# RWKV-7 block inverses: 64-column products and transposes in place of the second product

## The reference

```python
def step(S, inp):
    r_t, w_t, k_t, v_t, a_t, b_t = inp
    sa = jnp.einsum('bhvk,bhk->bhv', S, a_t)
    S = S * w_t[:, :, None, :] + sa[..., None] * b_t[:, :, None, :] + v_t[..., None] * k_t[:, :, None, :]
    return S, jnp.einsum('bhvk,bhk->bhv', S, r_t)
```

## Time and profile before

| | |
|---|---|
| median of 3 runs | 1586.68 us (1586.61 to 1587.28) |
| the profiled execution, its own time | 1589.47 us |
| its span, first to last instruction | 1587.7 us |
| PE busy | 1506.8 us, 95% |
| PE weight loads busy | 1377.6 us, 87% |
| DVE / ACT busy | 980.5 us / 697.7 us |
| stretch of the 24 steps | about 158.75 to 257 us of the span |

### The profile page before, as it was taken

One profiled execution on the slowest core, in us unless ns is written; L12 is line 12 of the kernel. 1 busy time (PEld: TensorE's weight loads), 2 busy tenths in 40 slices (PEclk: granted clock), 3 DMA queues, 4 the chain that ended last, 5 costly groups with the idle time before them and its releaser, 6 DMA issues. The chain is left out here.

```text
span 1587.7 us, 26386 instructions
## 1 busy us (share of the span) xinstructions
PE 1506.8 (95%) x10462; PEld 1377.6 (87%) x10462; DVE 980.5 (62%) x1605; ACT 697.7 (44%) x1125; POOL 55.5 (3%) x85
## 2 busy tenths in 40 slices
PE   6889999999999999999889999999999998899998
PEld 6786899789999899989868999989998987699997
DVE  4775464776666766664357766676665454576665
ACT  5461445454434433456345443353443445454343
POOL 1021000000000000000000000000000000000000
PEclk9999999999999999999989999999999899999999
DMA  7331200165543554433405555445454331165440
GB/s 312 120 120 45 115 2 1 43 264 198 196 173 147 199 196 174 186 120 143 176 1 199 204 193 198 175 163 199 180 199 159 132 144 56 40 239 199 182 174 27
DMA packets 24640, 237.88 MB, mean 150 GB/s; under 512 B 2528, under 2 KB 4720, under 8 KB 5744
## 3 DMA queue, kind: packets, MB, share of 16 engines
q1 hardware_dynamic: 22032, 233.46, 39.1%
q10 hardware_dynamic: 2528, 3.32, 0.6%
HBM read 235.70 MB, written 1.07 MB: 149 GB/s over the span
## 5 line engine op out<-in xcount | busy, mean ns | idle before, releaser
L375 PE MATMUL ps<-uT_h,w_gu 128*128 128x256 f32 x3520 | 614.3, 280 | 0.3 <-DVE w_gu L1677 0.2
L375 PEld LDWEIGHTS ps<-uT_h,w_gu 128*128 128x128 f32 x3520 | 537.7, 188 | 11.1 <-issue 1.6
L375 PE MATMUL ps<-uT_l,w_gu 128*128 128x256 f32 x1760 | 478.8, 279 | 0.0
L375 PE MATMUL ps<-w_dn,h_r 128*128 128x512 f32 x1320 | 326.3, 396 | 3.3 <-DVE h_r L1716 2.2
L375 PEld LDWEIGHTS ps<-uT_l,w_gu 128*128 128x128 f32 x1760 | 325.5, 188 | 0.0
L375 PEld LDWEIGHTS ps<-w_dn,h_r 128*128 128x128 f32 x1320 | 239.4, 188 | 54.5 <-issue 4.9
L1119 ACT CAST w_gu<-ring 128x2048 fp32r<-128x2048 f32 x110 | 209.9, 1908 | 158.5 <-PE ps L375 157.4
L1677 DVE TENSOR_TENSOR w_gu<-ring,w_gu 128x2048 fp32r<-128x2048 f32 x110 | 252.1, 2292 | 36.0 <-ACT w_gu L1119 36.0
L1707 DVE TENSOR_TENSOR us<-ps,bc 128x256 f32<-128x256 f32 x110 | 46.6, 423 | 205.2 <-PE ps L375 205.1
L375 PE MATMUL ps<-wk 128*128 128x128 f32 (+4 forms) x940 | 145.4, 301 | 15.3 <-ACT wk L1239 3.8
L1132 ACT ACTIVATE wk<-wk 128x256 f32<-128x256 f32 x110 | 46.1, 419 | 256.5 <-DVE wk L1705 256.5
(11 more groups left out here) (325 smaller groups left out, 1808.4 us busy)
## 6 DMA issues: line engine op xcount, KB each, us to landing
ring<-wstream SPq DMA_DIRECT2D x145, 1536.0 KB, 6.3
cst<-consts_in SPq DMA_DIRECT2D x1, 2057.0 KB, 15.6
wk<-t_row ACTq DMA_DIRECT2D x1, 2048.0 KB, 7.9
wk<-masks_in SPq DMA_DIRECT2D x1, 1152.0 KB, 25.7
x<-x_in SPq DMA_DIRECT2D x2, 512.0 KB, 4.6
inh<-gains ACTq DMA_DIRECT2D x2, 512.0 KB, 8.5
out_dram<-x SPq DMA_DIRECT2D x4, 256.0 KB, 2.2
cst<-consts_in ACTq DMA_DIRECT2D x1, 146.0 KB, 4.3
```

Source lines behind the costliest of these rows:

```text
L375: return pe.matmul(o, l, r, start=start, stop=stop, skip_group_check=True)
```

## The change

The first product streams only 64 of M's 128 columns, those of the even blocks of the level, and writes them side by side into 256 columns of bank 0; ACT copies 256 columns. The product for `Mm` is formed from these 64 columns, and DVE puts it into the even blocks' columns of `Mm`. The product for `Mt` is gone at five of the six levels. In its place PE transposes the updated `Mm` of the quad one step later, in steps q = 1 to 20, and DVE copies the transposes over `Mt` without a mask. At the last level (q = 20 to 23) only `Mt` is needed: its one 64x64 block comes from a product with 64 weight columns and 64 moving columns, and a plain copy. Two semaphores are new, `MT_ps` (PE to DVE, transposes done) and `Mt_ready` (DVE to PE, copy done).

```diff
+LAST_LEVEL = (LEVELS - 2) * QUADS
+        def blocks(a, q):
+            return a.rearrange("p (j w n) -> p j w n", w=2, n=2 << q // QUADS)
+        def evens(a, j, q):
+            return a[:, 64 * j:64 * j + 64].rearrange("p (j n) -> p j n", n=2 << q // QUADS)
...
                     for j in range(4):
-                        last = mm(ps[0][:, j * P:(j + 1) * P], AA4[k][:, j, 0:P], Mm[:, 4 * k + j, :])
+                        last = mm(evens(ps[0], j, q), AA4[k][:, j, 0:P], blocks(Mm[:, 4 * k + j, :], q)[:, :, 0, :])
...
-                    if q // QUADS < LEVELS - 2:
+                    if q >= QUADS:
+                        pe.wait_ge(s["Mt_ready"], q - QUADS + 1)
+                    for j in range(4):
+                        if q < LAST_LEVEL:
+                            last = mm(evens(ps[1], j, q), Mt[:, 4 * k + j, :], evens(Pb[:, q % 2, :], j, q))
+                        else:
+                            last = mm(ps[1][0:64, 64 * j:64 * j + 64], Pb[:, q % 2, 64 * j:64 * j + 64],
+                                      Mt[:, 4 * k + j, 64:128])
+                    last.then_inc(s["dM_ps"], 1)
+                    if 1 <= q <= LAST_LEVEL:
+                        if q >= 2:
+                            pe.wait_ge(s["Mt_ready"], q - 1)
                         for j in range(4):
-                            last = mm(ps[1][:, j * P:(j + 1) * P], Mt[:, 4 * k + j, :], Pb[:, q % 2, j * P:(j + 1) * P])
-                        last.then_inc(s["dMm_ps"], 1)
-                    for j in range(4):
-                        last = mm(ps[2][:, j * P:(j + 1) * P], Pb[:, q % 2, j * P:(j + 1) * P], Mt[:, 4 * k + j, :])
-                    last.then_inc(s["dM_ps"], 1)
+                            last = pe.transpose(ps[2][:, j * P:(j + 1) * P], Mm[:, 4 * ((q - 1) % QUADS) + j, :], ident)
+                        last.then_inc(s["MT_ps"], 1)
...
-                    A(act.copy(Pb[:, q % 2, :], ps[0][:, :]), "P_ev")
+                    A(act.copy(Pb[:, q % 2, 0:256], ps[0][:, 0:256]), "P_ev")
...
-                    if lv < LEVELS - 1:
-                        v.wait_ge(s["dMm_ps"], q + 1)
-                        V(v.copy_predicated(Mm[:, qs, :], mask(lv).unsqueeze(1).to_broadcast([P, 4, P]),
-                                            ps[1][:, :].rearrange("p (u n) -> p u n", u=4)))
                     v.wait_ge(s["dM_ps"], q + 1)
-                    V(v.copy_predicated(Mt[:, qs, :], mask(LEVELS + lv).unsqueeze(1).to_broadcast([P, 4, P]),
-                                        ps[2][:, :].rearrange("p (u n) -> p u n", u=4)), "M_ready")
+                    if q < LAST_LEVEL:
+                        new = ps[1][:, 0:256].rearrange("p (u j n) -> p u j n", u=4, n=1 << lv)
+                        V(v.copy_predicated(Mm[:, qs, :].rearrange("p u (j w n) -> p u j w n", w=2, n=1 << lv)[:, :, :, 0, :],
+                                            blocks(mask(lv), q)[:, :, 0, :].unsqueeze(1).to_broadcast(list(new.shape)), new),
+                          "M_ready")
+                    else:
+                        V(v.tensor_copy(Mt[0:64, qs, 64:128], ps[1][0:64, 0:256].rearrange("p (u n) -> p u n", u=4)),
+                          "M_ready")
+                    if 1 <= q <= LAST_LEVEL:
+                        before = 4 * ((q - 1) % QUADS)
+                        v.wait_ge(s["MT_ps"], q)
+                        V(v.tensor_copy(Mt[:, before:before + 4, :], ps[2][:, :].rearrange("p (u n) -> p u n", u=4)),
+                          "Mt_ready")
```

More of the change, by code:

```diff
@@ L103, in build @@
                  "bonus_read pads_ready eye_ready csm_ready e_ready scan_in ab_ready tok_ps tok_ev id_ready A_ps Mm_ps "
-                 "A_read P_ps P_ev dMm_ps dM_ps M_ready rhs_ps rhs_ev sa_ps sa_ev y_ps s_ps y_ev s_ev var_ready "
+                 "A_read P_ps P_ev dM_ps M_ready MT_ps Mt_ready rhs_ps rhs_ev sa_ps sa_ev y_ps s_ps y_ev s_ev var_ready "
                  "grs_ready yn_ready ynT_ps ynT_ev cmp_z cmp_h cmp_row cmp_hT cmp_hact cmp_kv cmp_ready "
```

## The result

The kernel after takes 1597.98 us (median of 4 runs, 1594.90 to 1599.47) against 1586.66 us before. The ratio is 1.0062, 95% interval [1.0047, 1.0077]: slower by some 10 us, where 14 us faster was forecast. Forecast and measurement part in one number: the mean granted clock of TensorE. In the profiled executions it was 0.981 before and is 0.962 after, and all four runs after lie between 0.962 and 0.967.

What follows compares the result with a forecast made beforehand. TensorE was taken to set the pace in the steps. Gains of 2.65 us (start), 10.5 (steps 5 to 19) and 1.0 (steps 20 to 23) sum to 14.1, so 1586.68 becomes 1572.6 us; range 1563 to 1581.

Steps and rivals of the forecast that it cites:

- The forecast's sum: Whole kernel: 2.65 us at the start, 10.5 in steps 5 to 19, 1.0 in steps 20 to 23; 14.1 us saved.
- rival D: In the 24 steps: half the columns streamed in the same time lower the clock; slower, say 1600 us; chance 0.05.
- D's price: Under rival D, a step at 1.2 GHz costs 4.9 us, or up to 6.4 if weight loads slow too.
- D's time: Under rival D, fifteen low steps lose 11 to 34 us, giving 1594 to 1617 us for the kernel.
- the forecast's rule that about five low steps eat the gain: Under rival D, the gain is gone once ten of fifteen steps run low at the small price, five at the large.
- What a pass costs: TensorE's products: the 128-column weight load sets a pass at 0.111 us, so streaming 64 moving columns shortens nothing.
- Rival B: First and Mm products: 64-column passes shorten to 0.069 us, 14 us more gained, 1558 us; chance 0.08.
- Second product out, transposes in: TensorE, each step: eight passes go (0.89 us), four transposes come (0.44 us); net gain 0.45 us.
- ScalarE's copy: Bank 0 copy of 256 columns instead of 512, 0.36 against 0.59 us; products come 0.25 us earlier a step.
- VectorE: Masked copy falls from 0.73 to 0.44 us, new unmasked copy takes 0.71; TensorE waits for neither, over 1.5 us spare.
- Rival C: In the steps: the gain passes to another wait (NSA units, copies, broken reads), half lost, 1580 us; chance 0.12.
- Steps 20 to 23: Last level: 64 weight columns save 0.34 us a step, step 20's transposes cost 0.44; 1.0 us gained together.

Runs made afterwards that it cites:

- the first experiment: Kernel after, but both products of steps 0 to 19 stream 128 columns again, the unused 64 thrown away; 1576.14 us, ratio 0.9917 to the kernel before.

## Why the prediction was wrong

The step that failed is the clock. The forecast's sum took a granted clock of 1.00 through the steps and put a fall at nothing; its rival D, "the clock falls in the steps", had a chance of 0.05. Measured, the clock was 0.50 from 160.9 to 215.5 us, and that cost 22.2 us, more than the 14.1 of the sum. D's mechanism was named as it then came: 64-column passes stream half the columns in the same time. It was set aside for two reasons, and neither bore on the place where the clock fell.

- *"from 259.8 to 272 us TensorE did mostly 64-column passes for 12 us and was granted 1.00".* True, and of the later 64-column steps it is true again (the last row of the table after, and the run with 128 columns in steps 0 to 7 only). It is a stretch without waits, it also had sixteen passes of 128 columns in it (from 262.70 us) and a few of 256, and it was compared with the steady steps. The fall came at 160.9 us, between the copies of steps 0 and 1 (158.75 and 162.47), where narrow passes meet the waits for ScalarE; TensorE was busy only 12.17 of 14.30 us there already before (158.7 to 173 us). That part was worked out for its time in the forecast and not for its clock.
- *"the gaps left in a step are some 0.1 us."* The gaps were taken as the only thing that drops the clock, after the fall at 288 us, and as what would have to last for it to stay down. It stayed down with TensorE busy 28.60 of 29.00 us. A pass fills as much busy time with 64 columns as with 128, so busy time could not show what was missing.

D's price was right at its upper end: "or up to 6.4" us a step, measured 6.52 in steps 6 and 7 (6.89 in step 8). The lower price of 4.9, with weight loads that keep their pace, did not come. D's time, 1594 to 1617 us, holds the measured 1597.98, but by luck in part: it counted fifteen low steps, and there were at most ten, at the high price. The copy of bank 0 of step 10 stands 57.42 us behind that of step 0 in the kernel after (158.75 to 216.17), and 35.21 us behind it with 128 columns in steps 0 to 7 (158.84 to 194.05). The low stretch costs 22.2 us. The spans of the two profiled executions are 24.2 us apart, 1597.5 and 1573.3, so nearly all of the difference is in it. That agrees with the forecast's rule that about five low steps eat the gain; here steps 1 to 10 were low at least in part.

The rest of the working can be checked where the clock was high:

- *What a pass costs:* right. 0.105 us for a 64-column pass in the kernel after (0.84 / 8) against the 0.111 taken, 4.07 against 4.13 us for a step when nothing but the columns is halved. Rival B is out.
- *Second product out, transposes in:* 0.45 us a step forecast, 0.50 measured (2.29 - 1.79).
- *ScalarE's copy:* 0.25 forecast, 0.27 measured (1.84 - 1.57); the copy takes 0.37 us. A step came to 3.36 us, 3.43 was forecast.
- *VectorE:* the masked copy 0.44 us from step 4 on (0.72 to 0.73 in steps 0 to 3) and the plain one 0.69, with no wait of TensorE for either, as forecast. Rival C did not occur.
- *Steps 20 to 23:* mis-sized. 1.0 us of gain was forecast; from the copy of step 20 to that of step 23 it was 11.68 us before (242.56 to 254.24) and is 11.80 after (250.40 to 262.20), with the clock at 1.00 in both. The narrow weights did nearly what was forecast: the eight passes with the two behind them take 0.93 us (259.40 to 260.33) where they took 1.22 (251.10 to 252.32), a gain of 0.29 for the 0.34. But from the NSA unit's transposes to the product it is now 0.42 us (258.98 to 259.40) and was 0.23, with 0.17 us in which weight loading waits for nothing that the trace shows. That leaves 0.1 us a step, and step 20 with its transposes lost 0.3. The forecast had no term for this pause, and no run shows what makes it.

```profile
258.98 0.26 PEld L809 LDWEIGHTS ps<-cst,wk 128*128 128x128 f32 x2
259.40 0.91 PEld L384 LDWEIGHTS ps<-wk 128*64 128x64 f32 x10 [0.17 <-issue]
260.33 0.63 PEld L384 LDWEIGHTS ps<-vsw,wk 128*128 128x128 f32 x4
```

- *The sum:* 14.1 us. The versions that hold the clock, with 128 columns throughout and in steps 0 to 7 only, gain 0.83% [0.61, 1.05] and 0.75% [0.53, 0.98], which is 13.2 and 11.9 us of 1586.7. In the profiled execution of the second it is 81.24 us from the copy of step 0 to that of step 23, and was 94.24 before: 13.0 us gained in the steps.

What stays open: what exactly tips the clock. The runs show that more streaming holds it and raises it, that narrow passes keep it down longer once it is down, and that with narrow products it can fall after a wait (kernel after, 160.9 us) and with no wait in front (kernel before with 64-column products, 239.5 us). They do not show why the same kernel falls in one run and not in the next, as that last version does, nor how much of the fall at 160.9 us is owed to the waits.

## What to carry to other kernels

Where the weight load sets the interval between matmuls, as here, fewer moving columns save next to nothing and can cost the clock. Try streaming the unused columns too, and save on the engine that copies the result. When a change thins out what TensorE streams, compare its streaming with that of a stretch of the same mix that lasts as long. Busy time does not help: it stayed near 100% here with the clock at half. A step at half clock is seen at once in the granted clock of its stretch, so look there before looking for a wait.

## What the runs showed of the hardware

- TensorE stayed at 1.2 GHz for over 100 us while it was busy 109.64 of 110.00 us; most of its passes there were weight loads of 128 columns with 64 or fewer columns streamed behind them.
- The granted clock can fall with no idle time in front: 9.30 of 9.30 us busy at 1.00, then 0.50 (kernel before with 64-column products).
- The interval of a pass with 128 weight and 64 moving columns in float32 goes from 0.105 us at 2.4 GHz to about 0.20 at 1.2 GHz, so a narrow pass is not spared by a low clock.
- VectorE's masked copy of 256 elements takes 0.44 us, but 0.72 to 0.73 in steps 0 to 3, where its runs are two elements long. The group of all twenty in the kernel after, by its minimum, median and maximum in ns:

```profile
L1879 DVE COPY_PREDICATED wk<-msk,ps x20: 428/439/726, 160.4 to 248.5; 128x256 f32<-128x256 uint8 x20
```

  ScalarE's copy of 256 elements out of PSUM takes 0.372 us in all twenty steps of the first experiment, whether in runs of two elements (steps 0 to 3) or longer, the same as a contiguous one.
